# VectorE's own convolution taps written into the PSUM bank ahead of TensorE's products

## The reference, cut to what matters

```
def conformer_conv(x, w_in, b_in, conv_w, conv_b, ln_g, ln_b, w_out, b_out):
    a, g = jnp.split(x @ w_in + b_in, 2, axis=-1)
    h = a * jax.nn.sigmoid(g)
    h = lax.conv_general_dilated(
        h, conv_w[:, None, :].astype(h.dtype), window_strides=(1,),
        padding=[(CONV_KERNEL - 1, 0)],
        dimension_numbers=("NWC", "WIO", "NWC"),
        feature_group_count=D_MODEL) + conv_b
    h = jax.nn.silu(layer_norm(h, ln_g, ln_b))
    return h @ w_out + b_out
```

## Time and profile before

| | |
|---|---|
| median of 3 runs | 1448.66 us (1447.51 to 1451.03) |
| the profiled execution's own time | 1448.54 us |
| its span, first to last instruction | 1446.7 us |
| mean granted TensorE clock | 0.996 |
| TensorE matmul busy | 1429.5 us |
| VectorE, ScalarE, GpSimd busy | 923.0, 613.0, 210.0 us |
| the stage of the change | about 914 to 1050 us of the span |

### The profile page before, as it was taken

The page is one execution under the profiler, slowest core; times in us unless marked ns, Lnnn a source line. Parts: engine busy times, 40 slices in busy tenths (PEclk is TensorE's granted clock), DMA queues, the critical chain, the costliest instruction groups (busy, mean ns, idle before and its releaser), DMA issues. The chain is left out here.

```text
span 1446.7 us, 19998 instructions
## 1 busy us (share of the span) xinstructions
PE 1429.5 (99%) x6884; PEld 1167.0 (81%) x6884; DVE 923.0 (64%) x1334; ACT 613.0 (42%) x911; POOL 210.0 (15%) x165
## 2 busy tenths in 40 slices
PE   9999999999999999999999999999899999999999
PEld 7788888888887898888888888666588888888887
DVE  7877773573655667767744756899888653544532
ACT  5544442342546665444432424676554322222210
POOL 7100000000302241000000004588411000000000
PEclk9999999999999999999999999999999999999999
DMA  5233233222421012332332322399713332232321
GB/s 191 88 101 102 92 99 114 76 101 89 123 101 59 30 60 88 101 102 87 102 116 73 101 98 91 102 208 233 173 45 102 116 102 89 100 102 87 102 95 51
DMA packets 50140, 148.07 MB, mean 102 GB/s; under 512 B 9376, under 2 KB 10144, under 8 KB 50080
## 3 DMA queue, kind: packets, MB, share of 16 engines
q1 hardware_dynamic: 47216, 138.36, 29.6%
q0 software_dynamic: 2016, 7.34, 2.8%
q10 hardware_dynamic: 848, 1.59, 0.3%
HBM read 137.21 MB, written 2.10 MB: 96 GB/s over the span
## 5 line engine op out<-in xcount | busy, mean ns | idle before, releaser
L610 PE MATMUL bank<-xh,whi 128*128 128x512 f32 x1184 | 465.3, 393 | 0.2
L612 PE MATMUL bank<-xh,wlo 128*128 128x512 f32 x1184 | 461.1, 389 | 0.0
L611 PE MATMUL bank<-xl,whi 128*128 128x512 f32 x1184 | 461.0, 389 | 0.0
L964 ACT ACTIVATE whi<-raw 128x1024 fp32r<-128x1024 f32 x244 | 255.8, 1050 | 254.1 <-PE bank L612 239.4
L1324 DVE TENSOR_TENSOR wlo<-raw,whi 128x1024 fp32r<-128x1024 f32 x230 | 288.7, 1256 | 42.9 <-ACT whi L964 34.8
L610 PEld LDWEIGHTS bank<-xh,whi 128*128 128x128 f32 x1184 | 222.5, 188 | 55.9 <-issue 6.8
L611 PEld LDWEIGHTS bank<-xl,whi 128*128 128x128 f32 x1184 | 222.6, 188 | 46.6 <-issue 1.0
L612 PEld LDWEIGHTS bank<-xh,wlo 128*128 128x128 f32 x1184 | 222.4, 188 | 46.3
L610 PE MATMUL bank<-ahi,whi 128*128 128x512 f32 x608 | 236.5, 389 | 0.0
L611 PE MATMUL bank<-alo,whi 128*128 128x512 f32 x608 | 236.5, 389 | 0.0
L612 PE MATMUL bank<-ahi,wlo 128*128 128x512 f32 x608 | 236.5, 389 | 0.0
(11 more groups left out here) (187 smaller groups left out, 1308.2 us busy)
## 6 DMA issues: line engine op xcount, KB each, us to landing
raw<-w_ffn_up SPq DMA_DIRECT2D x88, 512.0 KB, 3.3
raw<-w_ffn_down SPq DMA_DIRECT2D x32, 512.0 KB, 3.2
raw<-w_mlp_up SPq DMA_DIRECT2D x32, 512.0 KB, 3.2
raw<-w_mlp_down SPq DMA_DIRECT2D x32, 512.0 KB, 3.3
raw<-w_ain SPq DMA_DIRECT2D x16, 512.0 KB, 4.9
raw<-w_ffn_down SPq DMA_DIRECT2D x16, 384.0 KB, 3.0
raw<-w_qkv SPq DMA_DIRECT2D x12, 512.0 KB, 3.4
shifted<-hc SPq DMA_DIRECT2D x20, 258.0 KB, 5.8
```

Source lines behind the costliest of these rows:

```text
L610: nc.tensor.matmul(out_, hi, mh, start=first, stop=False)
L611: nc.tensor.matmul(out_, hi, ml, start=False, stop=False)
L612: return nc.tensor.matmul(out_, lo, mh, start=False, stop=last)
L964: nc.scalar.activation(whi[:, s, 0:tiles * P], raw[:, s, 0:tiles * P], ACT.Copy)\
```

## The change

Tables: the taps of the chunks 0, 1 and 4 move between the engines. TensorE's stay 86 in all, but the chunks 0 and 1 take 6 instead of 8 and only two shifted windows, so that they need 2 DMAs each instead of 4 and 3 rounds instead of 2; chunk 4 takes 12 instead of 8 taps, 3 rounds instead of 2. GpSimd's and ScalarE's rise from 65 to 72. VectorE's own go from 11, 10, 8, 6, 3, 2, 4, 11 to 12, 7, 3, 2, 1, 3, 3, 11, its late ones from 42 to 48. Units 6 to 9 leave `ADDED`: VectorE splits them. Units 17, 18 and 19 are prepared by ScalarE behind the last chunk's products and added by GpSimd behind the last chunk's sum.

Code: VectorE's own taps of all chunks but the last (`APART`) are written into TensorE's bank first, and TensorE adds its products to them; so `convolve(c)` waits for all own taps of the chunk (`tap_steps`), and `collect` has one addition less. Two more matmuls ahead of the stage open the banks 6 and 7. In the last chunk the second of the two shifted copies is issued by ScalarE, `diagonals` and `gated` are moved ahead, and `gated(7)` stands ahead of `collect(5)`.

```diff
--- before.py
+++ after.py
@@ -40,8 +40,9 @@
 FF_PARTS = (8, 8, 6)
 MLP_PARTS = (8, 8, 8, 8)
 TAPS = 31
-PE_TAPS = (8, 8, 8, 8, 8, 12, 20, 14)
-SHIFTS = (4, 4, 4, 4, 4, 4, 4, 2)
+PE_TAPS = (6, 6, 8, 8, 12, 12, 20, 14)
+SHIFTS = (2, 2, 4, 4, 4, 4, 4, 2)
+APART = C - 1
 GROUP = tuple(P // s for s in SHIFTS)
 ROUNDS = tuple(n // s for n, s in zip(PE_TAPS, SHIFTS))
 SPREAD = {s: (SHIFTS.index(s), C - SHIFTS[::-1].index(s)) for s in set(SHIFTS)}
@@ -49,14 +50,14 @@
 QUADRANT = P // 4
 GATE_AT = 8
 DIAGS = 2
-POOL_TAPS = (10, 9, 9, 8, 8, 8, 7, 6)
-LATE_TAPS = (2, 4, 6, 9, 12, 9, 0, 0)
+POOL_TAPS = (11, 10, 10, 9, 9, 9, 8, 6)
+LATE_TAPS = (2, 8, 10, 12, 9, 7, 0, 0)
 LATE_START = (2, 2, 2, 0, 0, 0, 0, 0)
 PARTS = 9
 GATE_PRODUCTS = 6
 HC = 3
-LOW_AT = {6: (0, 7), 7: (0, 9), 8: (1, 5), 9: (1, 7), 10: (2, 5), 11: (2, 7), 12: (3, 5), 13: (3, 7), 14: (4, 5),
-          15: (4, 7), 16: (5, 6), 17: (6, 5), 18: (7, 1), 19: (7, 5)}
+LOW_AT = {10: (2, 5), 11: (2, 7), 12: (3, 5), 13: (3, 7), 14: (4, 5), 15: (4, 7), 16: (5, 6), 17: (7, 5), 18: (7, 5),
+          19: (7, 5)}
 ADDED = tuple(LOW_AT)
 SLOTS = 4
 AHEAD = 3
@@ -333,6 +334,9 @@
         qb, qs = pbs, q_scale
         dist = cst[:, CST_DIST:CST_DIST + 2 * P]
+        def own_taps(c):
+            return range(PE_TAPS[c] + POOL_TAPS[c], TAPS - LATE_TAPS[c])
+
         def o_at(t, s):
             pr, n, ih = STEPS[s]
@@ -478,7 +482,7 @@
                 sp.wait_ge(hc_ready, c + 2)
                 if c >= 2:
                     sp.wait_ge(conv_done, c - 1)
-                for g in range(SHIFTS[c]):
+                for g in range(SHIFTS[c] if c < C - 1 else 1):
                     window = hc[g * group:(g + 1) * group, c % HC, 0:n]
                     taps = bass.AP(window.tensor, window.offset, [window.ap[0], (1, SHIFTS[c]), (1, n)])
                     sp.dma_start(shifted[:, c % 2, g, 0:n], taps).then_inc(hc_shifted[c % 2], 16)
@@ -633,6 +637,9 @@
                         if norm_name == "ain":
                             sum_features(norm_name, 1)
                     pe.wait_ge(xl_ready, X[norm_name] + t + 1 + (C if norm_name == "ffn1" else 0))
+                    if name == "ain" and t == 0:
+                        for b in range(2):
+                            nc.tensor.matmul(bank[6 + b][:], whi[:, 0, 0:P], xh[:, 0, :], start=True, stop=True)
                     w = slice(t * P, (t + 1) * P)
                     for k in range(n):
                         mm = three(acc[k][:], whi[:, k, w], wlo[:, k, w], xh[:, t, :], xl[:, t, :],
@@ -877,12 +884,15 @@
                 pe.wait_ge(diag_ready, c + 1)
                 if c >= 2:
                     pe.wait_ge(hv_ready, c - 1)
+                if c != APART:
+                    pe.wait_ge(tap_steps, sum(len(own_taps(e)) for e in range(c + 1)))
                 for q in range(ROUNDS[c]):
                     for g in range(SHIFTS[c]):
                         rows, at = slice(g * group, (g + 1) * group), SHIFTS[c] * q
                         mm = nc.tensor.matmul(bank[6 + b][rows, :], dg[:, c % DIAGS, q, rows],
                                               shifted[:, b, g, at:at + T],
-                                              start=(q == 0), stop=(q == ROUNDS[c] - 1))
+                                              start=(q == 0 and c == APART), stop=(q == ROUNDS[c] - 1),
+                                              skip_group_check=True)
                 mm.then_inc(conv_done, 1)
             def statistics(c):
@@ -1269,6 +1279,13 @@
             split_hi(p.unit, 0, AHEAD + 1)
             for c in range(C):
                 act.wait_ge(hc_ready, c + 2)
+                if c == C - 1:
+                    group, n = GROUP[c], PE_TAPS[c] - SHIFTS[c] + T
+                    act.wait_ge(conv_done, c - 1)
+                    for g in range(1, SHIFTS[c]):
+                        window = hc[g * group:(g + 1) * group, c % HC, 0:n]
+                        taps = bass.AP(window.tensor, window.offset, [window.ap[0], (1, SHIFTS[c]), (1, n)])
+                        act.dma_start(shifted[:, c % 2, g, 0:n], taps).then_inc(hc_shifted[c % 2], 16)
                 products(c, range(2))
                 if 2 <= c < C - 1:
                     square(c - 2)
@@ -1286,10 +1303,11 @@
                         negate_high(e)
                     for e in range(2 * (c + AHEAD) + (c > 0), min(2 * (c + AHEAD) + 2, 2 * C + 1)):
                         split_hi(p.unit, 0, e)
-                        negate_high(e)
+                        if e in ADDED:
+                            negate_high(e)
                 if c == C - 1:
                     square(c - 2)
-                for e in {C - 2: (17, 18), C - 1: (19,)}.get(c, ()):
+                for e in (17, 18, 19) if c == C - 1 else ():
                     split_hi(p.unit, 0, e)
                     negate_high(e)
             nc.scalar.activation(eps[:, 4:5], eps[:, 0:1], ACT.Sqrt)
@@ -1666,20 +1684,20 @@
             p = ph["ain"]
             V.memset(hc[:, :, 0:TAPS - 1], 0.0).then_inc(hc_ready, 1)
-            def own_taps(c):
-                return range(PE_TAPS[c] + POOL_TAPS[c], TAPS - LATE_TAPS[c])
-
             def late_taps(c):
                 return range(TAPS - LATE_TAPS[c], TAPS)
             def own_tap(c, n, k):
                 x, w = hc[:, c % HC, k:k + T], v("conv_w", c * TAPS + k)
+                at = taps[:] if c == APART else bank[6 + c % 2][:]
                 if n == 0:
-                    V.tensor_scalar(taps[:], x, w, None, ALU.mult).then_inc(tap_steps, 1)
+                    if 2 <= c != APART:
+                        dve.wait_ge(hv_ready, c - 1)
+                    V.tensor_scalar(at, x, w, None, ALU.mult).then_inc(tap_steps, 1)
                     return
                 dve.wait_ge(tap_steps, sum(len(own_taps(j)) for j in range(c)) + n)
-                V.scalar_tensor_tensor(hv[:, c, :] if n == len(own_taps(c)) - 1 else taps[:], x, w, taps[:],
+                V.scalar_tensor_tensor(hv[:, c, :] if c == APART and n == len(own_taps(c)) - 1 else at, x, w, at,
                                        op0=ALU.mult, op1=ALU.add).then_inc(tap_steps, 1)
             def late_tap(c, n, k):
@@ -1709,11 +1727,11 @@
                 part = prod[:, c % 2, :]
                 dve.wait_ge(tapped_steps, sum(POOL_TAPS[:c + 1]) - c - 1)
-                if own_taps(c):
+                if c == APART:
                     dve.wait_ge(tap_steps, sum(len(own_taps(j)) for j in range(c + 1)))
                     V.tensor_tensor(hv[:, c, :], part, hv[:, c, :], ALU.add).then_inc(own_added, 1)
                     part = hv[:, c, :]
-                    dve.wait_ge(own_added, sum(1 for j in range(c + 1) if own_taps(j)))
+                    dve.wait_ge(own_added, 1)
                 dve.wait_ge(late_steps, sum(LATE_TAPS[:c + 1]))
                 dve.wait_ge(conv_done, c + 1)
                 V.tensor_tensor(hv[:, c, :], bank[6 + c % 2][:], part, ALU.add).then_inc(hv_ready, 1)
@@ -1722,8 +1740,6 @@
                 k = 2 * (c % 2) + j
                 dve.wait_ge(chain_done, p.chain + 2 * c + j + 1)
-                if j and c:
-                    dve.wait_ge(tap_steps, sum(len(own_taps(e)) for e in range(c)))
                 V.tensor_tensor(taps[:] if j else tmp[:, k, :], acc[k][:], rinv[:], ALU.mult).then_inc(acc_free, 1)
             def gated(c):
@@ -1755,7 +1771,8 @@
                     evict(0, 0)
                 if c < C - 1:
                     gated(c)
-                diagonals(c)
+                if c < C - 1:
+                    diagonals(c)
                 own, late = own_taps(c), late_taps(c - 1) if c else []
                 rounds = max(len(own), LATE_START[c] + len(late))
@@ -1772,10 +1789,11 @@
                         own_tap(c, n, own[n])
                     if 0 <= n - LATE_START[c] < len(late):
                         late_tap(c - 1, n - LATE_START[c], late[n - LATE_START[c]])
+                if c == C - 2:
+                    diagonals(C - 1)
+                    gated(C - 1)
                 if c:
                     collect(c - 1)
-                if c == C - 2:
-                    gated(C - 1)
             collect(C - 1)
             dve.wait_ge(rms_ready, RR["ain"] + 2)
             V.reciprocal(r1[:], r1[:]).then_inc(rinv_ready, 1)
```

## The result

The changed kernel takes 1456.42 us, the median of 8 runs (1453.18 to 1458.0), beside 1450.03 for the kernel before (8 runs). The ratio is 1.0041, 95% interval 1.0032 to 1.0051: slower by 6 us, where I forecast no change, and 1456.42 lies outside my range of 1445.5 to 1453.0. I had started from the first three runs of before, 1448.66; with eight the baseline is 1.4 us higher, and what is left to explain is 6.4 us over before where I had 0.6. Run again later beside other experiments (e14) it took 1453.74, ratio 1.0021 (1.0009 to 1.0034). Both are slower; the size of the loss is 3 to 6 us.

The account below looks back on a forecast made before the run. TensorE, busy 1429.5 of 1446.7 us, was taken as the bound. Chunk 6's start +1.5, earlier gating -0.3, ScalarE's tail -1.0 and clock +0.5 gave +0.7 on 1448.54: 1449.2 us, range 1445.5 to 1453.0.

Parts of the forecast that it names:

- Chunks 2 to 6: Middle chunks: VectorE, ScalarE and GpSimd keep under TensorE's 13.4 us a chunk; shifted work priced at 0.
- The slow clock at chunk 0: 1.2 GHz behind chunk 0's wait: 1.7 us as behind other idle times, so 0 change; ends -1.7 and +1.7.
- rival C: Slow clock at chunk 0 twice as long, +1.7, chunk 1's own taps late, up to +2: 1451 to 1453; chance 0.17.
- The clock behind the idle time at the squares: Tail: TensorE waits for ScalarE's square of chunk 6, then 1.2 GHz in the layer norm: +0.5 us (0 to 1.7).
- The second issuer: Chunk 7's copies: ScalarE issuing one saves 0.6 us of issue time; total unchanged, as ScalarE decides the path.
- The wait at chunk 0: TensorE waits for VectorE's own taps ahead of chunk 0's convolution: 5.9 us instead of 2.3, +3.6.
- Chunk 1's wait and slow clock: At chunk 1 the wait of 3.42 us and the slow clock of 1.7 both go: -5.1 us.
- Chunk 7's wait: TensorE's idle time ahead of chunk 7's convolution shrinks from 2.6 us to about 1.
- ScalarE's squares: Last chunk: ScalarE's products, pairs and squares end 14.05 us behind the gated rows, on the longest path to the moments.
- A: Stage wins: slow stretch passes within chunk 0's wait, chunk 4's wait goes, no slow layer norm: 1446.4 us; chance 0.2.
- B: Output projection's low parts, units 17 to 19, land late: 1452.2 us at a landing of 16 us; chance 0.12.
- D: Convolution stage: the copies were not what TensorE waited for; held excluded by the releasers, no chance given.

Follow-up runs that it names:

- e14: The changed kernel run again, unchanged, beside later experiments: 1453.74 us, ratio 1.0021 to the kernel before.
- e8: Changed kernel with GpSimd's sums of tap products over 64 of 512 tokens, the other 448 left out: 1450.14 us, ratio 1.0007 to the kernel before.
- e1: Changed kernel with units 6 to 9 given back to GpSimd's adding DMAs, so VectorE doesn't split them: 1452.51 us, ratio 1.0019 to the kernel before.
- e13: Changed kernel with both of the last chunk's shifted copies issued by SyncE: 1451.2 us, ratio 1.0017 to the kernel before.
- e15: e1 with both of the last chunk's shifted copies issued by SyncE: 1449.94 us, ratio 0.9992 to the kernel before.
- e3: Changed kernel with chunk 0's own taps summed apart from TensorE's bank: 1451.49 us, ratio 1.001 to the kernel before.
- e9: Kernel before with only the last chunk's second issuer and its diagonals and gating ahead of `collect(5)`: 1450.16 us, ratio 1.0006 to the kernel before.
- e7: Changed kernel with units 6 to 9 back in adding DMAs, units 17 and 18 back in chunk 6, chunk 0's own taps apart: 1452.37 us, ratio 1.0017.

## Why the prediction was wrong

**The step that failed** is "Chunks 2 to 6": "dependent chains of up to 12 late taps: 12 x 0.76 + 1.2 + 0.6 + 0.7 = 11.6 us at most, under 13.4", and "I price all this at 0, covered by TensorE's chains". Three things were wrong in it.
- It counted a late chain and one split, not the engine's whole work of a chunk. For chunk 2 that is 3 own and 8 late taps, two splits, two evictions, a collect, gating and diagonals: 11 x 0.76 + 2 x 1.22 + 2 x 0.69 + 0.69 + 0.75 + 0.43 = 14.05 with all taps at 0.76, about 13.6 as e8 ran it (13.83 less 0.2 of waiting). TensorE takes 13.85. So nothing was left, where before VectorE waited 1.32 and 0.59 us for the two chains of this chunk.
- It took the split at 1.2 us, the row of one that met no sum. Beside GpSimd's sums, of which the change has seven more, the same instruction takes 1.6 to 2.3. This gave the 2.6 us (e8). It could have been read before: of the three splits of the stage in the trace of before only one took 1.22, and one, which rows 4 leave out, stands at 2.46:

```profile
941.83 2.46 DVE L1324 TENSOR_TENSOR wlo<-raw,whi 128x1024 fp32r<-128x1024 f32 x1
```
- The sum over the stage, -0.9 us, miscounted the own taps: they fall by 13 (55 to 42), not by 7, and the late ones rise by 6, so the taps give (-13 + 6) x 0.76 = -5.3, not -0.8, and the sum is -5.4. Measured is -0.4 for the whole span; diagonals alone take 8.27 us in place of 5.68. Even the right sum says nothing on a chunk in which nothing is left.

I had written that "without that cover a chunk would be late by a microsecond or less". In the first profile it was late by 2.5, with the slow clock behind it 4.3 us: the largest part of the 6.1 us by which I missed chunk 6's start. In the profiles e1 and e8 each remove it, by fewer splits or by no collision. In e14's profile the stretch to chunk 4 costs 3.7; how much it costs in the median is not settled: against the changed kernel's two medians e1 gives back 0 to 3 us, e8 2 to 5. The other term at nothing without a reason was the copies' time, taken as it was before: at chunk 4 it gave +0.9.

**Terms of the wrong size.** The slow clock at chunk 0, put at no change with 1.7 as upper end: +1.18 (2.04 less the round of 0.86); the first half of rival C happened, less than its 1.7. The size is partly luck: the stretch from chunk 0 to 1 takes 16.67 us here, the longest, and 15.64 to 16.39 in the six other profiles with the same wait of 5.94 or 5.95. In e1, the shortest, the 1.2 GHz began 3.1 us ahead of the wait's end, here 1.0. The clock behind the idle time at the squares, +0.5 with 1.7 as upper end: in the first profile 0.8 ahead of the moments (token sums 1.87 us, were 1.05) and 1.4 behind them, which I had left out by "nothing behind it changes"; in e14 nothing. The second issuer: I had its 0.6 us in ScalarE's queue and its 0.6 saved at the copies in the sum, but did not draw the conclusion that on the path that decides it only costs (e13, e15).

**What held.** The wait at chunk 0, 5.9 forecast, 5.95 measured, released by the own taps, and its origin, since e3 removes it. Chunk 1's wait and slow clock gone (-4.24, -4.23). A round costs 0.86, with two groups as with four: a round more at chunk 4 (four groups) cost 0.89, and three rounds take 2.80 at chunk 1 (two groups) and 2.78 at chunk 4. Chunk 7's wait about 1: 1.28. ScalarE's squares at 14.05 behind the gated rows: 13.76, and they decide the tail.

**Rivals.** A did not happen; only a part of the slow stretch lay in the wait (1.0 us). B did not: no wait for `wlo` at the projection. C, which ended at 1453, was the nearest; its clock half came, its late taps at chunk 1 not. D did not: the copies were what TensorE waited for, and it does again at chunk 3.

**Open.** What decides whether the clock falls behind an idle time of 0.2 to 2.0 us in the tail. Why the same four copies take 11.0 to 14.8 us. And how much of the 3 us between the two sets of the changed kernel is the chip and how much the collisions of its executions.

## What to carry to other kernels

Where work is moved between engines in a pipeline of chunks, add up the receiving engine's whole list for each chunk and set it against the chunk's time; a total over the stage hides the one chunk that is full. Price an instruction by its rows at the place where it will stand: for VectorE with two SBUF operands that means beside GpSimd, where here a split took up to 1.9 times and the diagonals 3.2 times as long. Then follow the next link as well: copies that start on time can still land late. A DMA issue put on a compute engine to save queue time costs that engine the same time (0.66 us here), so look first at which engine ends the stretch.

## What the runs showed of the hardware

- A VectorE subtraction of 128x1024 from two SBUF operands takes 1.22 us alone and 1.6 to 2.3 beside GpSimd's sums; diagonals of 128x256 take 0.43 and 1.38, an addition of 128x512 0.68 and, in e9, 2.30. VectorE instructions with one PSUM operand did not change.
- The 1.2 GHz stretch around the end of chunk 0's wait of 5.95 us lasted 6.8 us, the one behind chunk 3's wait of 2.51 us 3.4 us.
- Behind nearly the same idle time (2.01 and 1.99 us) the same program had 6.7 us at 1.2 GHz in one execution and none in another.
- From gated rows to landing, the same four copies of chunk 3 took 11.0 us (e13) to 14.8 us (e7).
